# Upward product of the feed-forward layers: high and low activations as one 512-column moving operand

## What is computed

```python
def conv_ffn(h, w_up, w_conv, b_conv, w_down):       # h: [1, 256, 1024]
    u = h @ w_up                                      # [1, 256, 5632]
    u = lax.conv_general_dilated(                     # per channel, 3 taps along the tokens
        u, w_conv[:, None, :], window_strides=(1,), padding=[(1, 1)],
        dimension_numbers=('NWC', 'WIO', 'NWC'), feature_group_count=u.shape[-1]) + b_conv
    val, gate = jnp.split(u, 2, axis=-1)              # 2816 channels each
    return (jax.nn.silu(gate) * val) @ w_down
```

## Time and profile before

| | |
|---|---|
| runs | 1055.84, 1056.65 and 1056.8 us, median 1056.65 us |
| profiled execution | span 1054.3 us from its first to its last instruction; its own device time isn't recorded separately, and the median lies 2.35 us above the span |
| TensorE matmul busy | 1030.4 us, 98% |
| VectorE busy | 849.4 us, 81% |
| ScalarE busy | 613.6 us, 58% |
| SyncE's queue | 153.44 MB, 45% of the 16 DMA engines' time |
| granted TensorE clock | 0.998 of full speed over the span |
| first feed-forward layer, the ten rounds | 154.2 to 327.0 us |
| second feed-forward layer, the ten rounds | 433.2 to 606.0 us |

### The profile page before, as it was taken

The page is one execution under the profiler, slowest core; times in us unless marked ns, Lnnn a source line. Parts: engine busy times, 40 slices in busy tenths (PEclk is TensorE's granted clock), DMA queues, the critical chain, the costliest instruction groups (busy, mean ns, idle before and its releaser), DMA issues.

```text
span 1054.3 us, 25164 instructions
## 1 busy us (share of the span) xinstructions
PE 1030.4 (98%) x10790; PEld 984.7 (93%) x10790; DVE 849.4 (81%) x1415; ACT 613.6 (58%) x878; POOL 18.3 (2%) x38
## 2 busy tenths in 40 slices
PE   7999999999999999999999999999999999999997
PEld 6999999999999989999999998889999988889997
DVE  7865689888879886998797797988998999965473
ACT  7744664444547666644444487556667667686443
POOL 2000000000000000000000000000000000000000
PEclk9999999999999999999999999999999999999999
DMA  9652266767554525476665636333323322234431
GB/s 280 212 183 94 81 220 220 239 221 237 189 198 151 170 70 175 165 247 218 232 238 195 205 122 199 115 90 120 122 85 118 121 83 81 82 122 158 162 121 41
DMA packets 135928, 168.21 MB, mean 160 GB/s; under 512 B 3200, under 2 KB 125056, under 8 KB 135584
## 3 DMA queue, kind: packets, MB, share of 16 engines
q1 hardware_dynamic: 131936, 153.44, 45.0%
q0 software_dynamic: 3904, 13.50, 3.4%
HBM read 164.83 MB, written 2.10 MB: 158 GB/s over the span
## 4 chain that ended last, share of the span: by engine, by line
PE 82%; DVE 12%; ACT 3%; DMA 2%; issue 1%; SPq 0%; DVEq 0%; ACTq 0%
PE bank L314 17%; PE bank L315 16%; PE bank L316 16%; DVE hf L2522 3%; PE banks L639 2%; PE banks L637 2%; PE banks L635 2%; PE bank L639 2%; PE bank L637 2%; PE bank L635 2%; DVE wl L300 2%; DVE wl L276 1%; PE bank L1175 1%; PE banks L1143 1%; PE bank L597 1%
## 5 line engine op out<-in xcount | busy, mean ns | idle before, releaser
L314 PE MATMUL bank<-xh,wh 128*128 128x256 f32 x1344 | 392.6, 292 | 0.0
L315 PE MATMUL bank<-xl,wh 128*128 128x256 f32 x1376 | 389.0, 283 | 0.0
L316 PE MATMUL bank<-xh,wl 128*128 128x256 f32 x1344 | 379.8, 283 | 0.0
L314 PEld LDWEIGHTS bank<-xh,wh 128*128 128x128 f32 x1344 | 256.9, 191 | 9.9 <-issue 3.6
L315 PEld LDWEIGHTS bank<-xl,wh 128*128 128x128 f32 x1376 | 263.5, 191 | 0.6 <-issue 0.5
L316 PEld LDWEIGHTS bank<-xh,wl 128*128 128x128 f32 x1344 | 257.1, 191 | 0.0
L276 DVE TENSOR_TENSOR wl<-raw,wh 128x2048 fp32r<-128x2048 f32 x95 | 216.8, 2286 | 42.9 <-ACT wh L271 42.7
L271 ACT ACTIVATE wh<-raw 128x2048 fp32r<-128x2048 f32 x95 | 181.0, 1906 | 38.9 <-PE bank L639 35.6
L300 DVE TENSOR_TENSOR wl<-raw,wh 128x1024 fp32r<-128x1024 f32 x86 | 103.6, 1217 | 15.1 <-ACT wh L292 15.0
L2522 DVE SCALAR_TENSOR_TENSOR hf<-big,vecs,hf 128x256 f32<-128x256 f32 x240 | 101.3, 477 | 0.0
L292 ACT ACTIVATE wh<-raw 128x1024 fp32r<-128x1024 f32 x86 | 87.5, 1058 | 11.2 <-PE bank L316 5.5
(11 more groups left out here) (424 smaller groups left out, 2226.6 us busy)
## 6 DMA issues: line engine op xcount, KB each, us to landing
raw<-in_ffn_w_up SPq DMA_DIRECT2D x44, 1024.0 KB, 5.1
raw<-in_w_in SPq DMA_DIRECT2D x36, 1024.0 KB, 5.4
raw<-in_ffn_w_down SPq DMA_DIRECT2D x22, 1024.0 KB, 5.1
big<-in_ada_w_t POOLq DMA_DIRECT2D x24, 512.0 KB, 5.2
raw<-in_gla_w_in SPq DMA_DIRECT2D x11, 1024.0 KB, 5.5
raw<-in_attn_w_qkv SPq DMA_DIRECT2D x6, 1024.0 KB, 4.9
raw<-in_gla_w_out SPq DMA_DIRECT2D x4, 1024.0 KB, 5.4
raw<-in_attn_w_out SPq DMA_DIRECT2D x4, 1024.0 KB, 5.2
```

What stands on the lines that cost most here:

```text
L314: nc.tensor.matmul(ps, wh, xh, start=start, stop=False)
L315: nc.tensor.matmul(ps, wh, xl, start=False, stop=False)
L316: return nc.tensor.matmul(ps, wl, xh, start=False, stop=stop)
```

## The change

- `XH` and `XL` become two halves of one tensor `XP` of shape [128, 2, 8, 256]. The other pairs are placed the same way (`GP`, `WP`, and the parts of `EARLY`), with no change in what uses them.
- PSUM banks 0 and 1 and banks 2 and 3 become pairs (`UPS[0]`, `UPS[1]`). Val goes to banks 0 and 1, gate to banks 2 and 3: each bank holds one half of 128 channels, with the sums of the high x in columns 0 to 255 and those of the low x in columns 256 to 511.
- A new `halved` takes the place of `product` for the 20 up blocks of the rounds in each layer: for each half and each tile one matmul of 512 columns (high weights by high and low x) and one of 256 (low weights by high x, onto the first 256 columns). 48 matmuls and weight loads become 32; the columns stay 768 for each pair.
- ScalarE's eviction (`take_hi`) reads only the first halves of the columns and signals `up_hi`. VectorE adds the second halves (`add_low`) and signals `evacuated`, which frees the banks.
- The centre tap with its bias moves from VectorE (four TENSOR_SCALAR in a round) to ScalarE (`centre`: two ACTIVATE for val and two for gate, with the column of the taps taken by a register inside the loop). It waits for `evacuated`. VectorE's `outer_taps` waits for `up_centred`.
- VectorE's order in a round becomes: `hidden`, `modulation`, low split, `add_low` of val, low part of the hidden values, low split, outer taps of val, `add_low` of gate, low split, outer taps of gate, `modulation` in odd rounds. ScalarE runs the tenth round outside its loop, without a centre tap for gate.
- The first gate block of each layer goes to bank 3 instead of bank 1 and waits for `rstd_ready`, since the sums of squares lie in that bank.
- Four semaphores that are used once become one counter (`zeroed`).

```diff
+        XP = sb("x_parts", [P, 2, KT, T], F32R)
+        XH, XL = XP[:, 0, :, :], XP[:, 1, :, :]
...
+        UPS = [ctx.enter_context(nc.psum_tensor(f"banks{2 * i}{2 * i + 1}", [P, 2, 512], F32))[:] for i in range(2)]
+        PS = [UPS[i // 2][:, i % 2, :] for i in range(4)]
...
+        def column(first, at):
+            return V[:, first + at:first + at + 1] if isinstance(at, int) else V[:, bass.ds(at + first, 1)]
...
+        def halved(pe, n, bank, i=0, ready=None):
+            pe.wait_ge(w_lo_ready, n + 1 + RING * i)
+            s = n % RING
+            for m in range(2):
+                ms = slice(m * P, (m + 1) * P)
+                for k in range(KT):
+                    if ready and m == 0:
+                        ready(k)
+                    nc.tensor.matmul(PS[bank + m].rearrange("p (a t) -> p a t", a=2), WH[:, s, k, ms], XP[:, :, k, :],
+                                     start=k == 0, stop=False, skip_group_check=True)
+                    last = nc.tensor.matmul(PS[bank + m][:, 0:T], WL[:, s, k, ms], XH[:, k, :], start=False,
+                                            stop=k == KT - 1, skip_group_check=True)
+            last.then_inc(block_done, 1)
...
                 def up(n, s, i=0, ready=None):
                     pe.wait_ge(evacuated, e0 + 2 * s - 1 + 2 * i)
-                    product(pe, n, 0, XH, XL, i, ready=ready)
+                    halved(pe, n, 0, i, ready=ready)
                     pe.wait_ge(evacuated, e0 + 2 * s + 2 * i)
-                    product(pe, n + 1, 1, XH, XL, i)
+                    halved(pe, n + 1, 2, i)
...
-                product(pe, n0 + 1, 1, *EARLY[2 * layer + 1])
+                pe.wait_ge(sem("rstd_ready"), 2 * layer + 2)
+                product(pe, n0 + 1, 3, *EARLY[2 * layer + 1])
...
+                def take_hi(half, n, i=0):
                     act.wait_ge(block_done, n + 1 + RING * i)
+                    act.wait_ge(sem("gate_convolved" if half else "val_convolved"), g0 + 1 + i)
+                    nc.scalar.activation(U[:, half, :, 1:T + 1], UPS[half][:, :, 0:T], ACT.Copy)\
+                        .then_inc(sem("up_hi"), 1)
+
+                def centre(half, i=0):
+                    taps, bias = (COL[name] + count * layer + 22 * half
+                                  for name, count in (("ffn_w_conv", 132), ("ffn_b_conv", 44)))
+                    act.wait_ge(evacuated, e0 + 3 + half + 2 * i)
+                    for m in range(2):
+                        at = 2 + m + 2 * i
+                        ins = nc.scalar.activation((CG if half else CV)[:, m, :], U[:, half, m, 1:T + 1], ACT.Identity,
+                                                   scale=column(taps + 44, at), bias=column(bias, at))
+                    ins.then_inc(sem("up_centred"), 1)
...
-                def turn(i, down_split):
+                def turn(i, down_split, last=False):
                     hidden_hi(layer, 0, i)
                     if not down_split:
                         split_hi(act, n0 + 4, i)
-                    take_val(n0 + 2, 1, i)
+                    take_hi(0, n0 + 2, i)
                     act.wait_ge(block_done, n0 + 2 + RING * i)
                     hidden_copy(layer, 0, i)
+                    centre(0, i)
                     split_hi(act, n0 + 5, i)
-                    take_gate(n0 + 3, 1, i)
+                    take_hi(1, n0 + 3, i)
                     split_hi(act, n0 + 6, i)
+                    if not last:
+                        centre(1, i)
 
                 turn(0, True)
-                with act.Fori(1, FI - 1) as i:
+                with act.Fori(1, FI - 2) as i:
                     turn(i, False)
+                turn(FI - 2, False, True)
...
+                def add_low(half, i):
+                    dve.wait_ge(sem("up_hi"), 2 * layer * (FI - 1) + 2 * i + half + 1)
+                    u = U[:, half, :, 1:T + 1]
+                    v.tensor_tensor(u, u, UPS[half][:, :, T:2 * T], ALU.add).then_inc(evacuated, 1)
...
                 def round_of(i):
+                    hidden(i)
                     split_lo(dve, n0 + 4, i)
-                    hidden(i)
-                    dve.wait_ge(evacuated, e0 + 3 + 2 * i)
-                    convolve(CV, 0, 1, ch, i)
+                    add_low(0, i)
+                    hidden_low(i)
                     split_lo(dve, n0 + 5, i)
-                    dve.wait_ge(evacuated, e0 + 4 + 2 * i)
+                    outer_taps(CV, 0, i)
+                    add_low(1, i)
                     if i < FI - 2:
-                        convolve(CG, 1, 1, ch, i)
+                        split_lo(dve, n0 + 6, i)
+                        outer_taps(CG, 1, i)
```

More of the change, by code:

```diff
@@ L200, in program @@
         PAIR = sb("pair_tiles", [P, 16, T])
-        GH = nc.alloc_sbuf_tensor_at("gh", [P, KT, T], F32R, offset=pair_at)[:]
-        GL = nc.alloc_sbuf_tensor_at("gl", [P, KT, T], F32R, offset=pair_at + KT * T * 4)[:]
+        GP = nc.alloc_sbuf_tensor_at("g_parts", [P, 2, KT, T], F32R, offset=pair_at)[:]
+        GH, GL = GP[:, 0, :, :], GP[:, 1, :, :]
         RAW = sb("raw", [P, RING, KT, BW])
-        WH = sb("wh", [P, RING, KT, BW], F32R)
-        WL = sb("wl", [P, RING, KT, BW], F32R)
+        WP = sb("w_parts", [P, 2, RING, KT, BW], F32R)
+        WH, WL = WP[:, 0, :, :, :], WP[:, 1, :, :, :]
         big_at = nc.sbuf_base + -nc.sbuf_base % 32
         BIG = sb("big", [P, 8, KT, T])
-        CYH, CYL, YH = (nc.alloc_sbuf_tensor_at(name, [P, KT, T], F32R, offset=big_at + tile * T * 4)[:]
-                        for name, tile in (("conv_y_hi", 55), ("conv_y_lo", 32), ("rwkv_y_hi", 8)))
-        EARLY = {0: [GH, GL]}
-        for i, tile in ((1, 0), (2, 44), (3, 0)):
-            if i < 3:
-                EARLY[i] = [nc.alloc_sbuf_tensor_at(f"early_{part}{i}", [P, KT, T], F32R,
-                                                    offset=big_at + (tile + KT * j) * T * 4)[:]
-                            for j, part in enumerate(("hi", "lo"))]
-            else:
-                EARLY[i] = EARLY[1]
+        CYP = nc.alloc_sbuf_tensor_at("conv_y_parts", [P, 2, 23 * T], F32R, offset=big_at + 32 * T * 4)[:]
+        CYL, CYH = (CYP[:, part, 0:KT * T].rearrange("p (k t) -> p k t", k=KT) for part in range(2))
+        CYP = CYP[:, :, 0:KT * T].rearrange("p a (k t) -> p a k t", k=KT)
+        YH = nc.alloc_sbuf_tensor_at("rwkv_y_hi", [P, KT, T], F32R, offset=big_at + 8 * T * 4)[:]
+        EARLY, EARLY_PARTS = {0: [GH, GL], 3: None}, {0: GP}
+        for i, tile in ((1, 0), (2, 44)):
+            parts = nc.alloc_sbuf_tensor_at(f"early_parts{i}", [P, 2, KT, T], F32R, offset=big_at + tile * T * 4)[:]
+            EARLY[i], EARLY_PARTS[i] = [parts[:, 0, :, :], parts[:, 1, :, :]], parts
+        EARLY[3], EARLY_PARTS[3] = EARLY[1], EARLY_PARTS[1]
         EARLY[4] = [nc.alloc_sbuf_tensor_at(f"early_{part}4", [P, KT, T + 2], F32R,
@@ L233, in program @@
         eps_rms, eps_ln, eps_gn, half_ln = (C[:, NCST - 4 + j:NCST - 3 + j] for j in range(4))
-        PS = [ctx.enter_context(nc.psum_tensor(f"bank{i}", [P, 512], F32))[:] for i in range(4)]
+        UPS = [ctx.enter_context(nc.psum_tensor(f"banks{2 * i}{2 * i + 1}", [P, 2, 512], F32))[:] for i in range(2)]
+        PS = [UPS[i // 2][:, i % 2, :] for i in range(4)]
         PSX = ctx.enter_context(nc.psum_tensor("banks45", [P, 2, 512], F32))[:]
@@ L511, in _ @@
                 .then_inc(sem("rank_landed"), 16)
-            pool.wait_ge(sem("w_up_zeroed"), 1)
+            pool.wait_ge(sem("zeroed"), 1)
             for j in range(4):
@@ L686, in normed_tile @@
                     pe.wait_ge(sem("rms_split"), k // 2 + 1)
-            pe.wait_ge(sem("u_zeroed"), 1)
+            pe.wait_ge(sem("zeroed"), 2)
             sums(0, first_ones)
@@ L2056, in hidden, with hidden_low @@
                         modulation_whole()
+                def hidden_low(i):
                     dve.wait_ge(sem("hidden_hi"), g1 + i + 1)
@@ L2059, in hidden, with outer_taps @@
                         .then_inc(sem("hidden_split"), 1)
+                def add_low(half, i):
+                    dve.wait_ge(sem("up_hi"), 2 * layer * (FI - 1) + 2 * i + half + 1)
+                    u = U[:, half, :, 1:T + 1]
+                    v.tensor_tensor(u, u, UPS[half][:, :, T:2 * T], ALU.add).then_inc(evacuated, 1)
+                def outer_taps(dst, half, i):
+                    dve.wait_ge(sem("up_centred"), layer * (2 * FI - 3) + 2 * i + half + 1)
+                    for j in (0, 2):
+                        for m in range(2):
+                            if j:
+                                ch.all(1)
+                            ins = v.scalar_tensor_tensor(dst[:, m, :], U[:, half, m, j:j + T],
+                                                         tap(j, half, 1, m, i), dst[:, m, :], ALU.mult, ALU.add)
+                            if j == 2 and m == 1:
+                                ins.then_inc(sem("gate_convolved" if half else "val_convolved"), 1)
```

(11 more changed lines are left out.)

23 lines of the change are left out of this document (6 added, 17 removed).

## The result

The changed kernel takes 1063.47 us, the median of 4 runs (1062.31 to 1064.34), beside 1056.35 us for the kernel before on the same chip: ratio 1.0067, 95% interval 1.0054 to 1.0079. It is slower by 7.1 us, 6.1 us more than forecast and outside the range.

What follows compares the result with a forecast made beforehand. TensorE bounded the kernel before; the VectorE-ScalarE loop was to become as slow and set each layer's end. Layer 0 at +0.2 us and layer 1's start at +0.5 gave +0.7 on 1056.65: 1057.4 us, range 1053.4 to 1061.4.

Steps and rivals of the forecast that it cites:

- chain at the layer's end and clock held: The main case: the path through VectorE and ScalarE sets each layer's end, TensorE keeps full clock; 1057.4 us, chance 0.42.
- Matmul term: TensorE's up blocks: 0.227 us per 512-column matmul, pair 0.360 to 0.347; 8.5 us available if TensorE stayed the bound.
- rival 3: 512 columns cost twice 256 on TensorE, so the matmul part gains nothing; 1059.0 us, chance 0.07.
- Loop: Path through VectorE and ScalarE between val additions: 16.50 us, 16.93 after odd rounds, nine steps 150.2 before the register.
- Centre pair: Two centre taps on ScalarE, on the loop's path: 0.80 us until the next instruction.
- Register: Address instruction before each centre tap in ScalarE's loop: 0.1 us a round taken, +1.0 us over ten rounds.
- Rival 4: The register in ScalarE's loop costs 0.3 us a round; 1061.4 us, chance 0.11.
- Layer's end: Last down block starts at 326.0 against 326.99, 1.0 us sooner; next product loses some 0.2; before the register.
- Clock: TensorE's clock was taken to hold through idle times of 3.3 to 4.3 us ahead of each last down block.
- Rival 2: TensorE's clock falls in the new idle time, 1.7 us a fall: 1059.1 for one, 1060.8 for two; chance 0.25.
- Rivals 1: TensorE stays the bound as the loop's steps overlap more: 1048.1 us for all, 1052.4 for half; chance 0.15.

Runs made afterwards that it cites:

- filled: The changed kernel with 24 matmuls of 256 columns, read by nothing, put ahead of each layer's last down block: 1059.88 us, ratio 1.0034.

## Why the prediction was wrong

Two steps of the prediction failed. The term for the two centre taps was 0.80 us and measured 1.00, which cost 3.9 us. And the forecast had the clock hold, at a price of nothing, through a wait of 3.3 us or more; it fell in both layers, which cost 3.6 us. Either alone, added to the forecast, would have left the time inside the range (1061.3 and 1061.0 us).

Four medians give the 7.1 us: 1055.99 without the bias (pair 0.82 us, no fall) is 0.4 below the kernel before; the second vector adds 3.9 (1059.88, filled, no fall); the two falls add 3.6 (1063.47). The step that I called the forecast, chain at the layer's end and clock held, was thus measured by itself: 1055.99 against the 1057.4 put down.

- **Matmul term: too good.** I took 0.227 us for 512 columns and 0.347 for a pair; it is 0.235 and 0.353. That leaves 640 x 0.0066 = 4.2 of 8.5 us, half way between the forecast and rival 3. (The 15.4 us that the text puts down for 0.213 us is a slip: by its own numbers it is 640 x 0.027 = 17 us.) The bounds from the plain float32 passes (no overhead at 512) didn't carry over. It made no difference to the time, as the text said: TensorE waits for the chain anyway. As for the 0.120 us of 256 columns, the section that the prediction cites (the Trainium skill, TensorE: Matmul & The Clock Gate, Back-to-back issue gap) gives its formula for an isolated matmul and says that it doesn't describe a stream in which each has its own weight load; the row is such a stream, so that the 120 ns don't speak against the formula.
- **Loop: right in its order and nearly in its size.** Forecast 16.50 and, after odd rounds, 16.93 us, with 0.1 each for the register; measured 16.77 and 17.07. Nine steps came to 151.98 us against 151.1. Most signatures came true: VectorE idle for 2.5 us on the high split behind the centre taps, TensorE idle for 3.1 us ahead of each last down block and 0.2 or less ahead of the others, released by the low part of the hidden values. The round of 17.07 lies just above the 16.7 to 17.0 forecast. That the 3.1 us came so near the 3.3 to 4.3 is in part luck: the chain came later than put down, and so did TensorE, with rounds 0.2 us longer.
- **Centre pair: the first step that failed.** "Two centre taps on ScalarE: 0.80 us, from two scaled copies of the same size". Those read a scale vector only; the centre taps read two. The timeline of ScalarE in the kernel before did have a row with both, outside the feed-forward layers, and I did not look for it:

```profile
627.88 1.09 ACT L1683 ACTIVATE big<-u,ln_rstd_tile,one_less_mu 128x256 f32<-128x256 f32 x2 [0.92 <-DVE u L2440]
```

  1.09 us for two against 0.91, which would have put the sum at +0.2 us a round, 4 us over both layers: 1061.4. From the first down block to the start of the last, the change takes 328.73 - 166.21 = 162.5 us, and 160.6 with the pair at 0.82: 1.9 us a layer, as the medians say.
- **Register:** 0.15 us a round against 0.1 taken, 1.2 us of wait a layer against 1.0. Rival 4 (0.3 us) did not hold; the sign that I named for it, more than 0.9 us between the first centre tap and the high split, did appear, but from the second vector. A bad sign, since it couldn't tell the two apart.
- **Layer's end: put a little too late.** With the pair as forecast the last down block starts 327.26 - 166.62 = 160.6 us after the first, in the kernel before 326.99 - 165.71 = 161.3; I had the two equal, and 0.7 us more in all for the next product and the second layer's start. Most of the difference lies in the nine steps of the loop, 315.47 - 165.19 = 150.3 us in that run against 151.1: those after odd rounds take 16.84 us where I had 17.03. That is 0.8 us in each layer; the 1.4 us by which 1055.99 lies below 1057.4 are not accounted for any closer.
- **Clock: the second step that failed.** Rival 2 held in full, in both layers, with 1.5 us a fall by the blocks' lengths and 1.8 by the medians, where 1.7 were put down. I gave it 0.25 and 1059.1 to 1060.8 us, though my own sum had TensorE idle beyond any gap that had kept the clock. The range's upper end left out a fall together with any mis-sized term, and both came. By the Trainium skill, TensorE: Matmul & The Clock Gate, HAM oscillation, waits between bursts of matmuls bring the array back to half clock; the trace agrees for the waits of 3.1 us (0.78 and 0.76 granted over the block that follows).
- **Rivals 1 and 3** did not hold: there is idle time at the layers' ends, and 512 columns are cheaper than twice 256, if only by 0.005 us (the sign named for rival 3 was 0.24 us, and 0.235 was measured).

## What to carry to other kernels

When work is moved to an engine with time to spare, look at what stands behind it in that engine's queue. Here a wait for VectorE was put ahead of a high split that VectorE needed next, and swapping two lines of ScalarE's order turned +7.1 us into -2.6. A term that stands on a loop is paid every round and may be paid again as clock at the end: price an operation from a row with the same operands, not only the same shape. And when a sum leaves TensorE idle longer than any gap in the trace that kept the clock, count the fall in the forecast.

## What the runs showed of the hardware

- An ACTIVATE of 128x256 takes 502 ns with a scale vector or a bias vector, and 595 ns with both. Copies of that size without either take 417 ns.
- A column chosen by a register delayed the first ACTIVATE behind a wait by 0.15 us, and not the second.
- TensorE's clock, with idle times as the profile counts them: after 2.9 us it fell to 1.2 GHz both times, for 3.41 us, once at the end of the wait and once 1.3 us into the work behind it. After 1.8 us it fell once of two times. After 1.63 us (kernel before) it held, as after 1.5 us (two times), 1.1 us (four) and 0.6 us (two). A fall cost a block of 48 matmuls 1.5 us.
- A reduced-format matmul of 512 columns takes 0.235 us beside 0.118 to 0.120 for 256, whether its columns lie in one piece or in two, 8 KB apart. Why it isn't nearer the 0.213 us of its columns is open.
